# Two token sets at the mixers' entry and exit norms, index projections tile by tile behind them, the store in eight pieces, and the layer norms' shift from two output tiles

## The reference

```python
# first block, i = 0, 1
h = swiglu(x, ...)                     # d_ff 2816
x = layer_norm(ALPHA * x + 0.5 * h, gain, bias)
m = pool_mixer(x) if i == 0 else dilated_attention_mixer(x)
x = layer_norm(ALPHA * x + m, gain, bias)
h = swiglu(x, ...)
x = layer_norm(ALPHA * x + 0.5 * h, gain, bias)
# second block, l = 0, 1
mod = silu(c) @ ada_w[l] + ada_b[l];  shift, scale, gate = split(mod, 3)
h = rms_norm(x, pre_norm[l]) * (1 + scale) + shift
p = h @ w_in[l]       # retention, sparse attention with an index (idx_q, idx_k), gated linear attention
y = (g0 * (ret @ w0) + g1 * (dsa @ w1) + g2 * (gl @ w2)) @ w_out[l]
x = x + gate * rms_norm(y, post_norm[l])
```

## Time and profile before

| what | value |
|---|---|
| median of 3 runs | 3653.62 us (3653.02 to 3654.09) |
| profiled execution's own time | 3652.63 us |
| its span, first to last instruction | 3650.8 us |
| mean granted TensorE clock | 0.974 |
| busy: PE, PEld, DVE, ACT, POOL | 94%, 77%, 40%, 23%, 68% |

### The profile page before, as it was taken

One profiled execution on the slowest core, in us unless ns is written; L12 is line 12 of the kernel. 1 busy time (PEld: TensorE's weight loads), 2 busy tenths in 40 slices (PEclk: granted clock), 3 DMA queues, 4 the chain that ended last, 5 costly groups with the idle time before them and its releaser, 6 DMA issues.

```text
span 3650.8 us, 47711 instructions
## 1 busy us (share of the span) xinstructions
PE 3426.7 (94%) x18252; PEld 2813.6 (77%) x18252; DVE 1462.7 (40%) x2239; ACT 855.8 (23%) x1508; POOL 2500.2 (68%) x2220
## 2 busy tenths in 40 slices
PE   7999979999999999989898999879999988999997
PEld 6887868888888887878777888757678766777875
DVE  6562553112311243251445110355656424565642
ACT  1110323110311033131333110232323212232321
POOL 7998767888788866537354888746566764646674
PEclk9999989999999999999999999989999998999998
DMA  5652222322233222112121232212222221222221
GB/s 189 193 182 97 79 81 70 103 89 95 81 94 98 92 86 81 59 47 93 47 70 47 92 94 96 93 59 74 58 70 64 87 87 59 64 66 73 61 90 58
DMA packets 321335, 312.02 MB, mean 85 GB/s; under 512 B 11504, under 2 KB 304016, under 8 KB 320912
## 3 DMA queue, kind: packets, MB, share of 16 engines
q1 hardware_dynamic: 303840, 277.91, 24.3%
q10 hardware_dynamic: 17328, 31.78, 2.7%
HBM read 307.56 MB, written 2.10 MB: 85 GB/s over the span
## 4 chain that ended last, share of the span: by engine, by line
PE 84%; DVE 7%; ACT 4%; issue 3%; POOL 1%; DMA 0%; ACTq 0%; DVEq 0%; SPq 0%; POOLq 0%
PE ps L385 49%; PE ps L1507 16%; PE ps L1267 4%; PE ps L557 3%; PE ps L532 2%; PE ps L1549 2%; PE ps L2074 1%; DVE at_sc L1179 1%; POOL wh L347 1%; PE ps L1887 1%; POOL wl L351 1%; PE ps L505 1%; ACT x L692 1%; PE ps L636 1%; PE ps L1858 1%
## 5 line engine op out<-in xcount | busy, mean ns | idle before, releaser
L347 POOL TENSOR_TENSOR wh<-w_raw,zero 128x512 fp32r<-128x512 f32 (+3 forms) x1108 | 1143.4, 1042 | 1109.0 <-PE ps L385 577.3
L351 POOL TENSOR_TENSOR wl<-w_raw,wh 128x512 fp32r<-128x512 f32 (+3 forms) x1108 | 1414.2, 1287 | 0.0
L385 PE MATMUL ps<-xh,wh 128*128 128x512 f32 x1968 | 772.1, 392 | 26.4 <-DVE xl L2425 19.6
L385 PE MATMUL ps<-xl,wh 128*128 128x512 f32 x1968 | 768.0, 390 | 0.0
L385 PE MATMUL ps<-xh,wl 128*128 128x512 f32 x1968 | 767.9, 390 | 0.0
L385 PEld LDWEIGHTS ps<-xh,wh 128*128 128x128 f32 x1968 | 370.9, 188 | 107.6 <-issue 22.7
L385 PEld LDWEIGHTS ps<-xh,wl 128*128 128x128 f32 x1968 | 370.7, 188 | 77.7
L385 PEld LDWEIGHTS ps<-xl,wh 128*128 128x128 f32 x1968 | 370.9, 188 | 77.1 <-issue 1.0
L1507 PE MATMUL ps<-xh,wh 128*128 128x512 f32 x688 | 291.8, 424 | 9.2 <-ACT stats L1649 6.4
L874 DVE TENSOR_TENSOR ps<-sg,ps 128x512 f32<-128x512 f32 x88 | 61.2, 696 | 588.8 <-PE ps L385 564.2
L1507 PE MATMUL ps<-xh,wl 128*128 128x512 f32 x688 | 273.0, 397 | 0.0
(11 more groups left out here) (331 smaller groups left out, 5986.4 us busy)
## 6 DMA issues: line engine op xcount, KB each, us to landing
w_raw<-in_w_in SPq DMA_DIRECT2D x120, 512.0 KB, 4.1
w_raw<-in_ffn_w_gate SPq DMA_DIRECT2D x88, 512.0 KB, 4.7
w_raw<-in_ffn_w_up SPq DMA_DIRECT2D x88, 512.0 KB, 4.7
w_raw<-in_attn_w_qkv SPq DMA_DIRECT2D x72, 512.0 KB, 4.5
w_raw<-in_ffn_w_down SPq DMA_DIRECT2D x64, 512.0 KB, 3.5
ada_raw<-in_ada_w ACTq DMA_DIRECT2D x24, 512.0 KB, 3.8
stats<-in_ada_w ACTq DMA_DIRECT2D x24, 512.0 KB, 4.1
w_raw<-in_ffn_w_down SPq DMA_DIRECT2D x32, 384.0 KB, 4.0
```

Source lines behind the costliest of these rows:

```text
L347: done.append(s["w_hi"].up(pool.tensor_tensor(hi[:, parts[q]], raw[:, parts[q]], zero, ALU.subtract)))
L351: s["w_lo"].up(pool.tensor_tensor(lo[:, parts[q]], raw[:, parts[q]], hi[:, parts[q]].bitcast(F32), ALU.subtract))
L385: mm = self.nc.tensor.matmul(out, a[:, slot, w], b(t), start=start and t == order[0] and q == 0, stop=stop and t == order[-1] and q == 2)
```

## The change

1. **Layer norm's shift** comes from two output tiles instead of four. The shift's product and the eight shifting operations stand two tiles earlier (in ffn 0 the ada work beside it too), and the sums of squares are taken in between the evictions, as the tiles come, instead of behind the last.
2. **Gain and bias.** VectorE's multiplication by 1/std takes the gain with it. ScalarE writes the high part in one activation with the bias, VectorE's low part adds the bias itself, and x keeps no bias; `act_complete` adds it (eight whole tiles) at the start of ScalarE's part of the next norm, and evictions wait for it.
3. **Mixer entry** (`pe_entry`, `dve_entry_tiles`, `act_entry_high`): squares, sum, root, reciprocal, multiplication, high and low parts are made in two token sets, and idx_q and idx_k are accumulated tile by tile behind the low parts, in halves. The eight squares go to TensorE one by one, not in pairs. Behind ffn 3 the second layer norm set stands behind the first entry set in the queues, and that norm takes a root and a reciprocal instead of Ln and Exp. The table DMAs are issued ahead of the first root, decay and lr_w behind the entry.
4. **Mixer exit** (`act_exit`, `dve_exit`): squares and sums of the first six tiles as they come; the last two tiles by `pe_last` in two sets, with sums in between.
5. **Store** in eight DMAs, two tiles of one set each.

```diff
-            logs=2, std_ready=2, centred=2 * KT, t_ready=2 * KT, x_ready=2 * KT, xh_ready=2 * KT, acts=2 * KT)
+            logs=2, std_ready=2, centred=2 * KT, t_ready=2 * KT, x_ready=KT, xh_ready=2 * KT, acts=2 * KT)
...
-        for m in range(4):
+        for m in range(2):
             ev(m)
...
+        self.wait_complete(dve, st, KT - 1)
+        dve.wait_ge(s["z_ready"].sem, st.at("z_ready", 2))
+        s["zsum_ready"].up(nc.vector.tensor_tensor(self.zsum[:], self.x[:, 0], self.x[:, 1], ALU.add))
         dve.wait_ge(s["mean_ready"].sem, st.at("mean_ready", 1))
         mean = self.ps[:, self.shift_bank(st)]
-        for n, m in enumerate((4, 5, 6, 7, 0, 1, 2, 3)):
...
+        for m in (*range(2, KT), 0, 1):
...
+        sums(0, self.x, 1)
+        for m in range(2, WHOLE):
+            ev(m)
+            if m > 2:
+                squared(m - 2)
+            dve.wait_ge(s["z_ready"].sem, st.at("z_ready", m + 1))
+            sums(0, self.x, m)
+        squared(WHOLE - 2)
+        squared(WHOLE - 1)
...
+    def act_complete(self, act, st):
...
+        for m in range(KT):
+            act.wait_ge(self.s["acts"].sem, st.at("acts", 0))
+            self.s["x_ready"].up(self.nc.scalar.activation(self.x[:, m], self.x[:, m], ACT.Identity, bias=self.ln[:, 1, u, m:m + 1]))
...
-            t = s["x_ready"].up(nc.scalar.activation(x, x, ACT.Identity, scale=self.ln[:, 0, u, m:m + 1], bias=self.ln[:, 1, u, m:m + 1]))
             if self.splits(st.kind, st.index):
-                act.wait_ge(s["x_ready"].sem, t)
                 hi, full, _ = self.split_views(st, m, h)
-                s["xh_ready"].up(nc.scalar.activation(hi, full, ACT.Copy))
+                s["xh_ready"].up(nc.scalar.activation(hi, full, ACT.Identity, bias=bias))
...
-            s["t_ready"].up(nc.vector.tensor_tensor(x, x, self.rstd(h), ALU.mult))
+            s["t_ready"].up(nc.vector.scalar_tensor_tensor(x, x, self.ln[:, 0, u, m:m + 1], self.rstd(h), ALU.mult, ALU.mult))
...
-            s["acts"].up(nc.vector.tensor_tensor(lo, full, high.bitcast(F32), ALU.subtract))
+            s["acts"].up(nc.vector.scalar_tensor_tensor(lo, full, self.ln[:, 1, u, m:m + 1], high.bitcast(F32), ALU.add, ALU.subtract))
...
+        tiles(0)
         for m in range(KT):
...
+            centre(m, 1)
+        invert(1)
+        dve.wait_ge(s["mod_ready"].sem, 2)
+        self.dve_entry_invert(dve, enter, 0)
+        self.dve_entry_tiles(dve, enter, 0)
+        tiles(1)
+        self.dve_entry_invert(dve, enter, 1)
+        self.dve_entry_tiles(dve, enter, 1)
...
+    def pe_entry(self, pe, st):
...
+        for h in range(2):
+            if h == 0 and before.kind == "ffn":
+                pe.wait_ge(s["centred"].sem, before.at("centred", 2 * KT))
+            for m in range(KT):
+                pe.wait_ge(s["e_sq"].sem, st.at("e_sq", KT * h + m + 1))
+                mm = self.nc.tensor.matmul(self.entry_mean(h), self.ones[:], self.half(self.squares[:, m], h), start=m == 0, stop=m == KT - 1)
+            s["e_var"].up(mm)
...
+            for step in range(KT + self.LAG):
+                for n, width in ((0, 256), (1, P)):
+                    k = step - self.LAG * n
...
+                    if n == 0:
+                        pe.wait_ge(s["acts"].sem, st.at("acts", KT * h + k + 1))
...
+                    for m in range(width // P):
...
+                        for q, (a, b) in enumerate(((self.wh, xh), (self.wh, xl), (self.wl, xh))):
+                            mm = self.nc.tensor.matmul(out, a[:, (c + n) % 2, w], b, start=k == 0 and q == 0, stop=k == KT - 1 and q == 2)
+                        if h == 1 and k == KT - 1:
+                            s["acc"].up(mm)
...
+    def act_entry_root(self, act, st, h):
+        s = self.s
+        act.wait_ge(s["e_var"].sem, st.at("e_var", h + 1))
+        s["e_root"].up(self.nc.scalar.activation(self.half(self.zsum, h), self.entry_mean(h), ACT.Sqrt, bias=self.eps[:, 2:3]))
+
+    def act_entry_high(self, act, st, m, h):
+        s = self.s
+        act.wait_ge(s["e_scaled"].sem, st.at("e_scaled", KT * h + m + 1))
+        s["xh_ready"].up(self.nc.scalar.activation(self.half(self.xh[:, m], h), self.half(self.mx_h[:, m], h), ACT.Identity,
+                                                   bias=self.mod[:, st.index, m:m + 1]))
+
+    def dve_entry_invert(self, dve, st, h):
+        s = self.s
+        dve.wait_ge(s["e_root"].sem, st.at("e_root", h + 1))
+        s["e_std"].up(self.nc.vector.reciprocal(self.entry_std(h), self.half(self.zsum, h)))
+
+    def dve_entry_tiles(self, dve, st, h):
...
+        for m in range(KT):
+            s["e_scaled"].up(nc.vector.scalar_tensor_tensor(self.half(self.mx_h[:, m], h), self.half(self.x[:, m], h), self.mod[:, n, KT + m:KT + m + 1],
+                                                            self.entry_std(h), ALU.mult, ALU.mult))
+            if m:
+                low(m - 1)
+        low(KT - 1)
...
+    def act_exit(self, act, st):
...
+        for m in range(WHOLE):
+            act.wait_ge(s["acc"].sem, self.acc(self.chunk_of(st, "out", m // 2), m % 2))
+            t = s["lin_ev"].up(nc.scalar.activation(self.mx_o[:, m], self.ps[:, m % 2], ACT.Copy, scale=0.5))
...
+            s["o_sq"].up(nc.scalar.activation(self.sq[:, m % 2], self.mx_o[:, m], ACT.Square))
+        self.act_then(act, nc.scalar.activation(self.eps[:, 5:6], self.ones[:, 0:1], ACT.Sqrt))
...
+    def dve_exit(self, dve, st):
...
+        tail(0, 0)
+        tail(1, 0)
+        invert(0)
+        for m in range(KT):
+            tile(m, 0)
             if m == 1:
                 tail(0, 1)
                 tail(1, 1)
...
+        invert(1)
...
+        self.dve_entry_invert(dve, enter, 0)
+        self.dve_entry_tiles(dve, enter, 0)
         for m in range(KT):
...
+            tile(m, 1)
+        self.dve_entry_invert(dve, enter, 1)
+        self.dve_entry_tiles(dve, enter, 1)
...
-                if (pair, part) == (2, 0):
+                if (pair, part) == (1, 0):
                     self.pe_shift(pe, st)
...
-        for mp in range(4):
-            self.pe_project(pe, st, "out", mp=mp, at=mp, before=self.x_tile(pe, st, 2 * KT) if mp == 0 else None)
-        self.pe_squares(pe, st, 1, 5)
+        for mp in range(3):
+            self.pe_project(pe, st, "out", mp=mp, at=mp, before=self.x_tile(pe, st, 3 * KT) if mp == 0 else None)
+        self.pe_last(pe, st, [(self.chunk_of(st, "out", 3), KT, None)], self.x_parts(), sums=self.pe_exit_sums)
+        self.pe_exit_sums(pe, st, 1)
...
+        for h in range(2):
+            for m in range(0, KT, 2):
+                sp.wait_ge(self.s["x_out"].sem, st.at("x_out", KT * (h - 2) + m + 2))
+                sp.dma_start(dst[:, m:m + 2, HALF * h:HALF * (h + 1)], self.x[:, m:m + 2, HALF * h:HALF * (h + 1)]).then_inc(self.out_done, 16)
```

408 lines of the change are left out of this document (254 added, 154 removed).

## The result

The changed kernel takes **3598.5 us** (median of five runs, 3597.2 to 3601.2) where the kernel before took 3653.6 beside it: ratio 0.985, 95% interval 0.9837 to 0.9864. The forecast was 3600, and it was the likeliest case that came. The profiled execution, the slowest of the five, took 3601.2 us, span 3599.4, against 3650.8: 51.4 us less. One execution of the kernel before in the second group of experiments took 4895 us at a mean granted clock of 0.65; the ratios leave it out.

The account below looks back on a forecast made before the run. TensorE, busy 94% of the span, was taken as the bound, so only its idle or late time could be won. 17.7 + 15.7 - 3 + 14 + 9 = 53.4 us off gave 3600 us as median, range 3584 to 3618.

Parts of the forecast that it names:

- Part 1, stage starts: Five next-stage starts behind norms that split: one ScalarE step less per tile makes them 17.7 us shorter in all.
- VectorE's scale (a two-input form with a scalar, same 0.33): Stage starts: taking the gain into VectorE's multiplication leaves its step at 0.33 us, a tile at 0.67.
- First tile: ready 0.6 us sooner: Stage starts: without one ScalarE step the first tile is ready 0.6 us sooner.
- Part 2, shift: Norms of pool and attention: shift from two tiles wins 9.5 and 8.5 us, less 2.3 for half clock: 15.7.
- Part 3, first entry: Mixer 0's entry: VectorE's last low part, ahead of its angle chain, ends later; 3 us slower, between 1 faster and 5 slower.
- Taken: 3 us slower: Mixer 0's entry: size chosen with the last low part at 2405.6 at half clock, 2400.7 at full, 2401.4 before.
- Part 4: Mixer 0's exit and mixer 1's entry: 14 us won after a new wait before ret_q; 9 to 20 by clock level.
- Part 5: Last mixer exit and store: last x tiles end at 3638.4 instead of 3647.6, 9 us won; store's landing taken as equal.
- The reciprocal: Half-width VectorE reciprocal at mixer entries and exits: 1.70 us taken, bounds 1.68 and 3.35; dear-price rival 3616 us, chance 0.12.
- only the first tile gains: Rival: VectorE under the split bounds the stage starts, which give 5.5 instead of 17.7 us: 3612 us, chance 0.13.
- The entries run at full level: Rival: no half clock at norms, mixer entries and exits; wins 2.3, 4, 6 and 1 us more: 3586 us, chance 0.20.
- The slower one: Rival: TensorE's many short waits drop it to 1.2 GHz for long: 3661 us and up, chance 0.05.

Follow-up runs that it names:

- warm: Changed kernel plus matmuls of ones, results unused, in TensorE's waits at four stage starts and both mixers' entries: 3588.4 us, ratio 0.9822.
- undo_shift: Changed kernel with the layer norm's shift taken from four output tiles again, square sums all behind: 3614.2 us, ratio 0.9896.
- angles: Changed kernel with both angle chains moved from behind VectorE's last low part into its waits for mixer 0's entry sums: 3596.7 us, ratio 0.9848.
- angles_one: Changed kernel with only the first angle chain moved into VectorE's wait for mixer 0's first entry sums: 3595.0 us, ratio 0.9836.

## Why the prediction was right

Predicted 53.4 us in the profiled execution, found 51.4; by the medians some 53.6 predicted, 55.1 found. Each mechanism was there, but that the sum came so near is in part luck: two terms were 4.0 and 2.4 us too hopeful, and three were 0.4, 2.1 and 1.0 too careful. Term by term ("in before's times" means shifted by what had been gained until then, so that both traces can be laid side by side):

- **Part 1, stage starts**: right in its mechanism, mis-sized. 17.7 predicted, 13.7 found (15.1 and 13.6 by the two ways of undoing it). By stretch 1.2, 4.3, 2.6, 4.2 and 1.4 against 3.4, 3.4, 3.6, 4.3 and 3.0. Two steps failed. "VectorE's scale (a two-input form with a scalar, same 0.33)" was wrong: the timeline gives 0.40 a step, so VectorE makes a tile in 0.79 us, not 0.67, and "so TensorE paces" doesn't follow from the prices. That cost little: TensorE is behind by then, and in four of the five second sets it runs without a gap (behind ffn2 a low part takes 0.67 and a tile 0.98, at VectorE's pace). The larger one is that the sum took 0.119 us a matmul throughout, with no term for the level. Pool's stretch, whose clock rose from 0.95 to 1.00, came out better than predicted; the two whose clock fell, behind ffn0 (0.95 to 0.89) and attention (1.00 to 0.94), fall shortest; and `warm`, all at 1.00, brings the sum to 146.8, under the predicted 148. The half level had been priced in the other parts and left out here.
- **"First tile: ready 0.6 us sooner"** failed where GpSimd's split runs: the low part came 0.5 us sooner, met the whole first step of the split and took 1.23 for 0.74. Behind pool, where the split starts later, TensorE's first product came 0.4 us sooner behind the last one (0.08 instead of 0.49).
- **Part 2, shift**: 15.7 predicted, 18.1 - 2.0 = 16.1 found, 15.6 when undone. The ffn norms' 2.0 us were not foreseen; `undo_shift` takes the half microsecond away at ffn0, and 0.3 of it shows as a wait for GpSimd's last split, beside which VectorE's additions now lie. The 2.3 set aside for half level did not come: the clock is 1.00 over pool's and attention's tails. What is left before the tail's sums is 1.9 and 2.1 us, for which 3 was said.
- **Part 3, first entry**: 3 us slower predicted, 5.4 found. That is more than the 5 us which the prediction itself named as a sign of being wrong, so for this term it was. The place and the cause were right: 7.7 + 7.1 us of waiting for ScalarE's copies behind the chain, which `angles` and `angles_one` show to be VectorE's. Of the wait for ik "longer, not shorter (some 13 us or more)" only the sum came true: it is split over iq and ik, and ik's own is 7.1, shorter than the 8.8 before. The step that failed is "Taken: 3 us slower": followed, the last low part ended at 2405.6, 4.2 later than in the kernel before. In before's times it ended at 2406.7, and of the 1.1 between, 0.4 lie ahead of the second reciprocal's end and the rest in the second set, 7.0 us for 6.2, whose 16 steps of the scalar form take 0.40 each and not 0.33.
- **Part 4**: 14 predicted, 16.1 found behind the half-level stretch. In before's times, the first index product came at 3003.5 (3006.1 predicted) and the split ended at 3041.0 (3042.6); the POOL wait is 6.3 us (5 predicted), the stretch at half level behind it costs the 1.9 of 2.0. The entries' own clock was better than priced: the second sets' sums ran at full level.
- **Part 5**: 9 predicted, 10.0 found: 9.4 to the last x tile and 0.6 by the store's smaller last piece, taken as equal.
- **The reciprocal** at half width: 1.76 us, 1.70 taken. The rule of the Trainium skill (VectorE: DVE Perf Modes, First, the fixed hardware budget) on the divide step would have given an estimated 2.1; the measurement decides. The activation table load is 1.28 us here too, and the next activation follows within 0.02 us where its input is ready, so the 2.7 of the Trainium skill (ScalarE: Activation LUTs, What ACT_TABLE_LOAD costs) and the 1 us made of it did not show.

Of the rivals, "only the first tile gains" was the wrong way round: the first tile gained least. "The entries run at full level" was half true: the second sets' sums did, and the rest of the second sets after some 3 us; `warm` made it so for both entries' sums and index products, by its clock of 1.00 there. The argument against it, "0.50 in all comparable stretches", was too strong from the start: the fifth start ran at 1.00 before. The slower one never came near: all that `warm` could take off the half level is 5.5 us in the starts, 5.4 at the first entry and 1.8 at the second, and much of it was there before; the rival needed 60 us of new cost.

## What to carry to other kernels

Before an operation is moved from one engine to another to relieve a queue, price it in the form that it will have (with a scalar it is 0.06 us dearer here) and at the moment at which it will run: half a microsecond sooner can mean that it meets GpSimd's work in full and ends no sooner. Where an engine's waits are cut into many short ones, carry the clock through every stretch of the sum, not through the long waits alone; a few matmuls without use in such waits were worth 10 us here, more than any of the three ways of moving the angle chain in VectorE's queue. And when a stretch is shortened on the engine that seems to wait, ask what its successor in the same queue is: at the first entry the order of the index products was worth 2.5 us at most, since the angle chain stood behind the last low part.

## What was not expected of the hardware

- TensorE was kept at full level by matmuls without use in its waits: 119 of them, two rows each in the profile, 29.6 us of their own, won 10 us. By the groups of `warm` (busy us, mean ns):
```profile
L487 PE MATMUL ps<-ones 128*128 128x128 f32 x238 | 29.6, 276 | 0.5 <-DVE squares L800 0.5
```
- A VectorE operation of 128x256 with a scalar from a tile takes 473 ns, the plain form 413, with one operand in PSUM in both. Beside GpSimd's split the low part goes up to 1.51 us, in either form by as much, while the scale, with one input in PSUM, stays at 0.46 to 0.48.
- In mixer 0 the stretch between TensorE's waits for `stats` and for `gf` takes 32.8 us in the changed kernel, at a granted clock of 0.80 in its first 8.7 us, and 34.1 in `angles`, at 0.67; the other traces have 32.6 to 34.2, though no edit touches it. Why it falls one way or the other stays open. By windows, the changed kernel and then `angles`:
```profile
2572.00:2580.67 8.67, 8.67 (x36) 6.61 (x37) 6.90 (x16) 3.13 (x9) 6.67 (x6) 0.80 0.32 82
```
```profile
2566.33:2575.00 8.67, 8.67 (x28) 6.62 (x30) 5.82 (x15) 2.53 (x8) 6.62 (x6) 0.67 0.31 82
```
